# Turning the inverses of a gated delta mixer: products with the identity against 32 by 32 squares on VectorE

## The reference, cut to what matters

```python
def gated_delta_chunked(q, k, v, g, beta):
    ...
    kk = jnp.einsum('bhnid,bhnjd->bhnij', k, k)
    L = jnp.where(strict, beta[..., :, None] * jnp.exp(jnp.where(strict, diff, 0.0)) * kk, 0.0)
    eye = jnp.eye(C, dtype=jnp.float32)
    rhs = jnp.concatenate([beta[..., None] * v, (beta * jnp.exp(b))[..., None] * k], axis=-1)
    sol = lax.linalg.triangular_solve(eye + L, rhs, left_side=True, lower=True, unit_diagonal=True)
    u, w = sol[..., :dv], sol[..., dv:]
    ...
```

## Time and profile before

| | us |
|---|---|
| runs | 2505.41, 2509.98, 2510.16 |
| median of the three | 2509.98 |
| the profiled execution | 2505.38 |
| its span | 2503.6 |
| PE busy in the span | 2424.4 (97%) |
| DVE, ACT, POOL busy | 1129.9, 581.8, 330.0 |

### The profile page before, as it was taken

One profiled execution on the slowest core, in us unless ns is written; L12 is line 12 of the kernel. 1 busy time (PEld: TensorE's weight loads), 2 busy tenths in 40 slices (PEclk: granted clock), 3 DMA queues, 4 the chain that ended last, 5 costly groups with the idle time before them and its releaser, 6 DMA issues. The chain is left out here.

```text
span 2503.6 us, 49492 instructions
## 1 busy us (share of the span) xinstructions
PE 2424.4 (97%) x19869; PEld 2195.0 (88%) x19870; DVE 1129.9 (45%) x1888; ACT 581.8 (23%) x1239; POOL 330.0 (13%) x345
## 2 busy tenths in 40 slices
PE   8999999999898899999999999999999999999898
PEld 6787787688444899999999999999999999999776
DVE  4667618635323523333344344344443434343485
ACT  4434324653112000001110111111111111111265
POOL 0000116252001000000010010010100101010230
PEclk9999997999998999999999999999999999999899
DMA  4111211000621866777788888899898988988562
GB/s 153 43 51 51 89 55 44 26 3 24 245 71 63 277 220 235 249 253 266 272 285 299 290 292 313 311 313 325 310 323 314 320 311 315 317 316 317 194 212 76
DMA packets 113983, 528.52 MB, mean 211 GB/s; under 512 B 15044, under 2 KB 38808, under 8 KB 64696
## 3 DMA queue, kind: packets, MB, share of 16 engines
q1 hardware_dynamic: 99160, 481.16, 54.7%
q0 software_dynamic: 14688, 45.37, 5.6%
HBM read 485.84 MB, written 40.63 MB: 210 GB/s over the span
## 5 line engine op out<-in xcount | busy, mean ns | idle before, releaser
L1886 PE MATMUL ex_psum<-ex_xT,weight_ring_a 128*128 128x134 f32 (+14 forms) x7168 | 900.4, 287 | 4.8 <-DVE ex_xT L1871 4.8
L1886 PEld LDWEIGHTS ex_psum<-ex_xT,weight_ring_a 128*128 128x128 f32 x7168 | 885.9, 192 | 6.3 <-issue 5.6
L1928 PE MATMUL ex_psum<-ex_hT,weight_ring_b 128*128 128x134 f32 (+14 forms) x4096 | 506.0, 286 | 0.0
L1928 PEld LDWEIGHTS ex_psum<-ex_hT,weight_ring_b 128*128 128x128 f32 x4096 | 503.0, 191 | 0.0
L1747 POOL DMA_INDIRECT ex_rows<-xn_dram,ex_list x170 | 164.7, 969 | 1368.2 <-DVE ex_list L1790 1317.4
L1896 DVE TENSOR_SCALAR ex_gate<-ex_psum,bias_gate_up 128x192 f32<-128x192 f32 x256 | 92.8, 404 | 526.4 <-PE ex_psum L1886 525.9
L1900 DVE TENSOR_SCALAR ex_up<-ex_psum,bias_gate_up 128x192 f32<-128x192 f32 x256 | 95.0, 413 | 379.1 <-PE ex_psum L1886 379.1
L1913 ACT ACTIVATE ex_sig<-ex_gate 128x384 f32<-128x384 f32 x128 | 66.9, 523 | 700.9 <-DVE ex_gate L1896 700.5
L1938 ACT ACTIVATE ex_yT<-ex_psum,bias_down 128x192 f32<-128x192 f32 x256 | 83.1, 436 | 564.6 <-PE ex_psum L1928 564.6
L2189 PE MATMUL project_psum<-n_hi,w_in_hi 128*128 128x512 f32 x464 | 187.0, 403 | 2.9 <-DVE n_lo L520 2.9
L2189 PE MATMUL project_psum<-n_lo,w_in_hi 128*128 128x512 f32 x464 | 181.6, 391 | 0.0
(11 more groups left out here) (347 smaller groups left out, 2475.5 us busy)
## 6 DMA issues: line engine op xcount, KB each, us to landing
weight_ring_a<-in_w_gate_up SPq DMA_DIRECT2D x224, 1024.0 KB, 5.5
weight_ring_b<-in_w_down SPq DMA_DIRECT2D x128, 1024.0 KB, 6.9
weight_ring_b<-in_w_gate_up SPq DMA_DIRECT2D x32, 1024.0 KB, 6.3
y_dram<-ex_y SPq DMA_DIRECT2D x80, 192.0 KB, 6.0
w_in_pieces<-in_w_in SPq DMA_DIRECT2D x29, 512.0 KB, 3.6
y_dram<-ex_y SPq DMA_DIRECT2D x52, 128.0 KB, 5.3
project_work<-in_x SPq DMA_DIRECT2D x8, 512.0 KB, 7.1
gates_dram<-project_work POOLq DMA_DIRECT2D x16, 256.0 KB, 2.9
```

Source lines behind the costliest of these rows:

```text
L1886: mm = pe.matmul(self.ps[:, bank, i * CAP:i * CAP + width], w[:, k, i * P:(i + 1) * P], self.xT[:, k, 0:width], start=(k == 0), stop=(k == ...
L1928: mm = pe.matmul(self.ps[:, bank, first:first + width], w[:, i, j], self.hT[:, k, 0:width], start=(k == 0 and j % 2 == 0), stop=(k == KT - ...
```

## The change: VectorE's transposes take the place of the turns

The turns on PE, their PSUM banks and the ACT copies go, both for the first inverses and for levels 1 to 4. DVE turns `inv_T` of a tile into `inv` with one `transpose` instruction over 128 by 256, which turns each 32 by 32 square where it stands. The first six of the first turns stand in DVE's tile loop, each at the end of a turn of it, two tiles behind; the last two follow the loop. In the level loop the turn of step s-1 stands behind the subtraction of step s. PE's first product waits for the whole tile loop of DVE, since banks 0 and 1 are then free.

```diff
-        cut0, inv0, first_turned, first_kept = sem("first_cut"), sem("inv_T_first"), sem("first_turned"), sem("first_kept")
-        cut, x_done, x_kept, z_done, z_used, t_done, t_kept = (sem(n) for n in (
-            "cut", "x_done", "x_kept", "z_done", "z_used", "inv_turned", "inv_kept"))
+        cut0, inv0, inv_turned = sem("first_cut"), sem("inv_T_first"), sem("inv_turned")
+        cut, x_done, x_kept, z_done, z_used = (sem(n) for n in ("cut", "x_done", "x_kept", "z_done", "z_used"))
...
-            for t in range(NT):
-                if t == 0:
-                    pe.wait_ge(prod, 4 * (NT - 1))
-                pe.wait_ge(inv0, t + 1)
-                if t >= 2:
-                    pe.wait_ge(first_kept, t - 1)
-                turn_by_chunk(TURN + t % 2, inv_T[:, t, :]).then_inc(first_turned, 1)
...
-            for s in range(N + 2):
+            for s in range(N + 1):
                 if s < N:
                     l, t = STEPS[s]
 
+                    if s == 0:
+                        pe.wait_ge(prod, 4 * NT)
                     pe.wait_ge(cut, s + 1)
-                    if s < NT:
-                        pe.wait_ge(first_kept, t + 1)
-                    else:
-                        pe.wait_ge(t_kept, s - NT + 1)
+                    pe.wait_ge(inv_turned, s + 1)
...
-                if s >= 2 and STEPS[s - 2][0] < LEVELS - 1:
-                    q = s - 2
-                    l, t = STEPS[q]
-                    pe.wait_ge(z_used, q + 1)
-                    if q >= 2:
-                        pe.wait_ge(t_kept, q - 1)
-                    turn_by_chunk(4 + q % 2, inv_T[:, t, :]).then_inc(t_done, 1)
...
-            for t in range(NT):
-                act.wait_ge(first_turned, t + 1)
-                act.copy(inv[:, t, :], ps[:, TURN + t % 2, 0:H]).then_inc(first_kept, 1)
...
-                if s >= 2 and STEPS[s - 2][0] < LEVELS - 1:
-                    q = s - 2
-                    act.wait_ge(t_done, q + 1)
-                    act.copy(inv[:, STEPS[q][1], :], ps[:, 4 + q % 2, 0:H]).then_inc(t_kept, 1)
...
+            def turn(t):
+
+                dve.transpose(inv[:, t, :], inv_T[:, t, :]).then_inc(inv_turned, 1)
+
+            def turn_first(t):
+                dve.wait_ge(inv0, t + 1)
+                turn(t)
...
+                if t >= 2:
+                    turn_first(t - 2)
+            turn_first(NT - 2)
+            turn_first(NT - 1)
             for s, (l, t) in enumerate(STEPS):
                 dve.wait_ge(z_done, s + 1)
-                if s >= NT and l < LEVELS:
-
-                    dve.wait_ge(t_done, s - NT + 1)
+                if s >= NT:
+                    dve.wait_ge(inv_turned, s - NT + 1)
                 dve.tensor_tensor(inv_T[:, t, :], inv_T[:, t, :], ps[:, 2 + s % 2, 0:H], ALU.subtract).then_inc(z_used, 1)
+                if s >= 1 and STEPS[s - 1][0] < LEVELS - 1:
+                    dve.wait_ge(z_used, s)
+                    turn(STEPS[s - 1][1])
```

More of the change, by code:

```diff
@@ L1021, in delta @@
             "out", "out_squares", "out_roots", "out_inverse", "out_normed", "out_turned", "out_kept"))
-        ROWS, QK, KN, VN, TURN = 0, 3, 4, 5, 6
+        ROWS, QK, KN, VN = 0, 3, 4, 5
         BROW, KK = [7, 1], [6, 2]
@@ L1093, in by_chunk @@
                 return mm
[L1095 to L1101, removed]
             ones = g.k[:, K_ONES:K_ONES + P]
@@ L1166, in _ @@
                     pe.wait_ge(z_used, N)
-                    pe.wait_ge(t_kept, N - NT)
                     pe.wait_ge(nat_done, 2 * NH * NT)
@@ L1259, in _ @@
                                    scale=small[:, BETA, t, h:h + 1]).then_inc(v_done, 1)
-            for t in range(NT):
-                act.wait_ge(first_turned, t + 1)
-                act.copy(inv[:, t, :], ps[:, TURN + t % 2, 0:H]).then_inc(first_kept, 1)
[L1263 to L1269, removed]
-                if s >= 2 and STEPS[s - 2][0] < LEVELS - 1:
-                    q = s - 2
-                    act.wait_ge(t_done, q + 1)
-                    act.copy(inv[:, STEPS[q][1], :], ps[:, 4 + q % 2, 0:H]).then_inc(t_kept, 1)
+            for s in range(len(STEPS)):
+                act.wait_ge(x_done, s + 1)
+                if s >= 2:
+                    act.wait_ge(z_done, s - 1)
+                act.copy(tmp[:, 2 + s % 2, 0:H], ps[:, s % 2, 0:H]).then_inc(x_kept, 1)
             for t in range(NT):
```

## The result

The changed kernel takes 2488.02 us (median of 4 runs, 2485.66 to 2489.44) against 2508.38 (4 runs, 2505.41 to 2510.16): a ratio of 0.9918, 95% interval 0.9903 to 0.9933, so 17 to 24 us gained. The forecast was 2493 us, with 16.9 gained. Of the 5.0 us between the two, 1.6 are the fourth run of the kernel before, which moved its median from 2509.98 down to 2508.38. The profiled execution took 2487.37 us with a span of 2485.6, 18.0 less than the span before.

The account below looks back on a forecast made before the run. PE was taken to bound the level loop. Turns 15.0, breaks 1.2 and earlier start 2.5 us gained, less 1.8 for the half clock, make 16.9 off 2509.98: 2493 us, range 2486 to 2504.

Parts of the forecast that it names:

- 32 turns off PE: Level loop, levels 1 to 4: each step falls from 1.40 to 0.93 us, as at level 5; 15.0 us gained.
- breaks in PE's supply: Level loop: short breaks in PE's instruction supply, 4.6 us, shrink with fewer instructions; 1.2 us gained (0 to 2).
- earlier first x, the tile loop's cost in it: Start of level loop: PE's first product comes 2.5 us earlier, after 0.6 us lost to six transposes in DVE's tile loop.
- half clock in the loop: First two level-loop steps: PE's clock, halved after a longer pause, returns after 3.6 us; 1.8 us lost (0 to 4).
- outside the stage: Solution and scan are the same code, and the whole rest moves up; no gain or loss counted.
- DVE's part: Level loop: a 0.62 us transpose per step, overlapped with the subtraction, needs 0.80 us under PE's 0.93; DVE stays hidden.
- DVE binds: Rival, level loop: subtraction and transpose do not overlap, steps take 1.08 us, gain 12.1 us, time 2498; chance 17%.
- POOL and DVE on SBUF: Rival: transposes cannot run beside POOL, level-loop steps take 1.17 us, tile loop loses 2.2; gain 7.0, time 2503.0; chance 12%.
- The third rival: PE's clock does not come back: level loop at half clock to its end, 35.4 us lost, 2528.5 us; chance 4%.

Follow-up runs that it names:

- PE unread, many: Changed kernel plus the old turn's 16 recorded PE products per step at levels 1 to 4, read by nobody; ratio 0.9986 to the kernel before.
- three transposes: Changed kernel plus two more unread 128x256 DVE transposes in each of 32 steps; ratio 0.9963 to the kernel before.
- turn behind scale: Changed kernel with the six transposes in DVE's tile loop moved behind the scaled identity; 2488.49 us, ratio 0.9924 to the kernel before.
- early start: Changed kernel with the level loop begun before the last tile's first inverse is done; 2486.32 us against 2488.94 for the changed kernel.

## Why the prediction was right

The mechanism was right. The sizes erred both ways, and that they nearly cancel is luck. By its own terms, in the profiled execution:

| term | predicted | measured |
|---|---|---|
| 32 turns off PE | -15.0 | -15.0 (1.40 to 0.93 us a step) |
| breaks in PE's supply | -1.2 | -3.1 (5.0 to 1.9) |
| earlier first x, the tile loop's cost in it | -2.5 | -2.0 (2.4 and 2.5 in two other traces) |
| half clock in the loop | +1.8 | +1.1 (2.4 in two other traces) |
| outside the stage | 0 | +1.0 (1.4 later at its start, 0.4 less behind it) |
| sum | -16.9 | -18.0 |

By medians the gain was 20.4 us, and 18.5 and 19.5 for the same kernel on two other chips, against 16.9 forecast.

*The turns.* Reading level 5 as the step without a turn held to the hundredth, and "PE unread, many" shows that nothing but PE's time was in it.

*The breaks* were the term most off, outside the bounds of 0 to 2 that it was given. I let them go in proportion to the instructions; they fell from 5.0 us to 1.9 by the spacing of the steps, which is what closes the sum. They were 0.2 to 2.0 us in the nine traces with steps of 0.93 us, and 2.3 to 5.0 in the three with steps of 1.40. The kernel before has one trace, and its 5.0 us are the most of all, so a part of the fall is the chance of that execution.

Their places are not chance. One break of the kernel before, in PE's timeline:

```profile
558.20 0.28 PE L1092 MATMUL dn_psum<-dn_inv_T,dn_tmp 64*64 64x64 f32 x2
558.78 0.62 PE L1092 MATMUL dn_psum<-dn_inv_T,dn_tmp 64*64 64x64 f32 x14 [0.31 <-issue]
```

Counted in recorded products from the first x, the breaks of the kernel before stand in front of numbers 350, 474, 598, 722 and so on to 1715, every 124 or 125. Those of the changed kernel stand in front of 476, 600, 848, 975, 1097 and 1221, on the same grid, with 724 left out; in its second and third trace they are on it too. The profile has a DMA queue of the kind "instruction"; packets, MB and share, before and after:

```profile
q8 instruction: 109, 1.79, 0.3%
q8 instruction: 105, 1.72, 0.3%
```

From first x to solution it moves 15 packets of 16 KB in the trace before and 10 in the one after, one for every such place. That PE waits there for its next block of instructions fits all of this, but no run shows it. Fewer instructions make fewer such places, 12 breaks before and 6 after; why each is smaller too, 0.31 us in the mean and not 0.42, stays open.

*DVE's part.* The transpose is 0.44 us, not the 0.62 that I took, because the rows came from a strided form; the lower bound was the right one. It changed nothing, since DVE was hidden either way, by some 0.26 us a step (0.93 - 0.67) and not 0.13. The overlap on which the margin rested is shown by "three transposes". So "DVE binds" fell: its premise was no overlap.

*POOL and DVE on SBUF.* Half right. The scaled identity did lose its 0.40 us to POOL and got it back, shown by "turn behind scale". The transpose itself does not conflict with POOL: 0.44 us with the cut beside it, and POOL's 0.73 unchanged. That rival fell. By the Trainium skill, "VectorE: DVE Perf Modes", section "Two Vector instructions with no wait between them", the second read interface is what the engines share; the traces agree: L1269, with two operands in SBUF, takes 1.09 us in place of 0.68 where it meets POOL, and the transpose, with one, stays at 0.44.

*The first x.* The prediction has 0.6 us for the tile loop. The stage's first tile ran 0.5 us later in this trace, before any transpose, and the tiles with one added about 0.5 us once and 0.07 each after that (4.94 us a tile against 4.87), so 2.0 us were left of 2.5. The late first tile varies between executions: the second scaled identity starts 6.0 us behind the stage's start here and 5.6 and 5.5 in the two other traces, and there the first x came 2.4 and 2.5 us earlier than before.

*The clock.* It came back, as forecast, but not at the fixed delay of 3.6 us into the work that the prediction took from rows 11: 2.9 us after the first x in this trace, and 5.9 and 5.8 in the two others. One of the two starts in rows 11 was misread as well. The turns began at 514.89, and 0.64 for 519.0 to 519.5 puts the return near 519.4, 4.5 us into the work. The third rival, a loop at half clock, did not come near.

## What to carry to other kernels

Look for the stretch of the same loop that already runs without the part you mean to remove: its rhythm is the answer, whatever the engine rows say. Before moving work to another engine, add up starts and not records, and ask of a row's duration whether its access pattern is yours. An earlier start behind a longer pause of TensorE can be worth nothing, since the clock takes it back; fill the pause with real work.

## What the runs showed that I had not expected

- A DVE transpose of float32 takes 1.04 ns a column contiguous and with the write at a stride of 2 elements, and 1.8 at a stride of 8, on the read or the write side alike.
- One 128x280 product between groups of 64x64 products lengthened the step by 0.81 us, where its columns at the rate of the 128x512 products (0.85 us each) make 0.47. The groups of 64x64 around it also stood 0.51 and 0.57 us apart, not 0.47.
- Executions of one program differ in TensorE's start: 1.1, 2.4 and 2.4 us lost to the half clock behind the same pause of 5.5 us.
- The short breaks in TensorE's supply stand at fixed places, one for some 124 recorded 64x64 products and their loads, and between 0 and 0.9 us are lost at each.
- TensorE's pauses of 1.3 and 1.4 us in the early start did not lower the clock; the pause of 5.5 us in the changed kernel did, and so did that of 2.8 us in the kernel before.
